# The first stage of a decoder step on one core: how the norm's weights arrive, which queue carries the small transfers, and where two row blocks are turned

## The chip, the core and the metric

The kernel runs on one core of a Trainium2 chip. The metric is the device time of one execution in microseconds (us). TensorE, VectorE, ScalarE and POOL (GpSimd) compute; SyncE, ScalarE and POOL issue DMA transfers, each on a queue of its own.

## The reference

One inference step of a hybrid decoder with 1024 prompt rows and 8 sampled sequences of 4 new rows, 1056 rows of width 1024 together. Only the beginning matters here:

```python
def rmsnorm(x, g):
    xf = x.astype(F32)
    y = xf * lax.rsqrt(jnp.mean(xf * xf, -1, keepdims=True) + EPS)
    return (y * g.astype(F32)).astype(x.dtype)
...
def mixer_inputs(x, g, w_in):
    B, T = x.shape[:2]
    proj = rmsnorm(x, g) @ w_in
...
def layer_tail(x, mix, w_out, g_mlp, w_up, w_down, g_ple, w_ple, w_ple_gate, p):
    x = x + mix @ w_out
```

The normed rows go through one projection, whose columns feed an attention group and a convolution group; behind them come output projection, MLP, an embedding term and a last norm. The raw `x` is needed again for the first residual.

## The kernel before

All is float32; a product is made of three matmuls of fp32r parts (high times high, high times low, low times high), so each operand is split into a high part (`..hi`, ScalarE) and a low part (`..lo`, VectorE here).

The first stage, function `front`, is one program per engine, in an order written out by hand; the engines meet at semaphores. The 1056 rows are nine blocks `x_rows0` to `x_rows8` (the last with 32 rows). For each block r: ScalarE squares and sums (`square`, L576) and takes the root (`root`, L581); VectorE makes the inverse and scales with the norm's weights `g_rows`, 128 partitions x 1024, into `xn` (`scale`, L1035, buffers of two); TensorE turns it in eight 128x128 transposes into the banks `ps_a` and `ps_b` (`side("xn..")`, L810); ScalarE copies the high part `Ahi` (`high`, L587) and VectorE subtracts the low part `Alo` (`low`, L1043), after which a bank is free.

`g_rows` is made on the chip: one row of 4 KB, `g_row`, is loaded, TensorE multiplies it with a column of ones (L862), and ScalarE copies the two banks (L678).

The projection has 19 tiles of 128 columns (`TILES`). Tile t is: weights `win_raw` loaded by SyncE (L179, one buffer), high part (L187), low part (L1083), 24 x 3 matmuls of 352 columns (L791), and an epilogue on ScalarE (or VectorE, L1078, for the kind "a"). Tiles 0 and 1 are run by thirds j of the rows, so that they begin when the first three blocks are turned; tiles 2 to 18 run whole. Into tiles 1 to 16 other turns are slotted, by the table `IN_TILE`: a `side` after the sixth, 13th and 20th group of matmuls.

The raw rows are also turned and sent to DRAM (`x_spill`) for the residual: eight transposes, two ScalarE copies and two DMA issues for each block (`keep_x`, L603 and L611). Blocks 6, 7, 8, 2, 3, 4, 5 use `ps_a` and `ps_b` within tiles 0 to 4 (`X_KEPT_ORDER`, `IN_TILE`). Blocks 0 and 1 are turned at the very start into banks that the projection needs only later (`first_rows`, L841); ScalarE copies them around the high part of tile 1's weights.

Fifteen small transfers (constants, page table, state rows, one pair of weights; the first is `g_row`) are issued by ScalarE before anything else (L557 to L569). TensorE turns the constants (L871 to L873) after the blocks 0 to 2, when nine of them have landed (`loaded`). VectorE, once it has `u`, works through 124 convolution taps between its other duties; POOL has its own taps for the sampled rows.

## Time and profile before

| | |
|---|---|
| median of 3 runs | 1925.12 us (1924.26 to 1925.91) |
| the profiled execution | 1924.49 us, span 1922.7 us |
| TensorE busy | 1845.2 us, 96% of the span |
| VectorE, ScalarE, POOL busy | 914.4, 664.1, 590.8 us |
| DMA | 163.67 MB, mean 85 GB/s |
| granted TensorE clock, mean | 0.985 of full |

The span runs from the first to the last instruction of the profiled execution. In rows of the profile a start is given in us from the beginning of the span, then a duration; rows of several instructions (x4) give the time that they cover. Names are those of the code without buffer numbers; L1035 is a line of the kernel. PEld is TensorE's weight load.

### The profile page before, as it was taken

What the parts mean: (1) busy time and instruction counts of PE and PEld (TensorE: products, weight loads), DVE (VectorE), ACT (ScalarE), POOL (GpSimd) and SP (SyncE); (2) the same over time, 40 slices, a digit from 0 to 9 for tenths busy, and PEclk for the clock granted to TensorE, in tenths of its full rate; (3) what the DMA queues carried; (4) which work ended last, traced back from release to release, by engine and by line L of the source; (5) the groups of instructions that cost most, each with busy time, mean ns of one, the idle gap of its engine ahead of it and who ended that gap; (6) DMA issues with size and microseconds to landing.
All of it is one profiled execution on the core that took longest, in us unless ns stands there. A gap on an engine that the chain in (4) does not pass through costs nothing.

```text
span 1922.7 us, 35068 instructions
## 1 busy us (share of the span) xinstructions
PE 1845.2 (96%) x13394; PEld 1724.5 (90%) x13394; DVE 914.4 (48%) x1622; ACT 664.1 (35%) x1249; POOL 590.8 (31%) x582
## 2 busy tenths in 40 slices
PE   7999998999988999999999999999999999999998
PEld 6999988999975767667999999999999999999898
DVE  5699965675538677766423221222221212124425
ACT  4312332345335666667222211121212121214335
POOL 0002962233214443434343222222222212125531
PEclk8999998999999999999999999999999999999999
DMA  5322455536322544441432111111111111112114
GB/s 159 91 62 59 108 173 139 137 105 160 97 90 62 146 128 122 122 133 56 135 109 76 34 44 44 45 44 55 34 55 39 50 40 50 39 45 94 50 39 135
DMA packets 195069, 163.67 MB, mean 85 GB/s; under 512 B 23157, under 2 KB 177474, under 8 KB 194384
## 3 DMA queue, kind: packets, MB, share of 16 engines
q1 hardware_dynamic: 176493, 139.11, 24.5%
q0 software_dynamic: 5568, 15.21, 3.1%
q10 hardware_dynamic: 12842, 7.09, 1.3%
q8 instruction: 111, 1.82, 0.4%
q14 instruction: 55, 0.44, 0.1%
HBM read 147.70 MB, written 18.25 MB: 86 GB/s over the span
## 4 chain that ended last, share of the span: by engine, by line
PE 30%; issue 25%; POOL 9%; DVE 4%; ACT 2%; POOLq 0%; DVEq 0%; ACTq 0%
PE ps L206 10%; POOL wm_lo L192 6%; PE ps L2219 5%; PE ps L2591 4%; PE ps L1663 2%; PE ps L1675 2%; PE ps L1652 2%; POOL S L1619 2%; DVE S L1919 1%; PE ps L1702 1%; PE ps L2608 1%; PE ps L1710 1%; ACT S L1802 1%; PE ps L1738 1%; DVE y_lo L2084 0%
## 5 line engine op out<-in xcount | busy, mean ns | idle before, releaser
L192 POOL TENSOR_TENSOR wm_lo<-wm_raw,wm_hi 128x512 fp32r<-128x512 f32 (+1 forms) x96 | 169.0, 1760 | 557.3 <-ACT wm_hi L187 557.3
L2408 DVE TENSOR_TENSOR xT<-ps,xT 128x1056 f32<-128x1056 f32 x64 | 80.5, 1258 | 260.1 <-PE ps L206 260.1
L1619 POOL TENSOR_SCALAR S<-S,inv,gate_p 128x64 f32<-128x64 f32 (+6 forms) x192 | 122.8, 657 | 195.7 <-DVE inv L1929 195.7
L187 ACT ACTIVATE wm_hi<-wm_raw 128x512 fp32r<-128x512 f32 (+1 forms) x96 | 73.9, 769 | 286.6 <-PE ps L206 286.6
L206 PE MATMUL ps<-Ahi,wm_hi 128*128 128x352 f32 x768 | 167.5, 326 | 4.5 <-POOL wm_lo L192 2.5
L206 PE MATMUL ps<-Hhi,wm_hi 128*128 128x352 f32 x768 | 167.3, 326 | 1.3 <-POOL wm_lo L192 1.3
L206 PE MATMUL ps<-Ahi,wm_lo 128*128 128x352 f32 x768 | 166.2, 324 | 0.0
L206 PE MATMUL ps<-Alo,wm_hi 128*128 128x352 f32 x768 | 165.8, 324 | 0.0
L206 PE MATMUL ps<-Hhi,wm_lo 128*128 128x352 f32 x768 | 165.6, 323 | 0.0
L206 PE MATMUL ps<-Hlo,wm_hi 128*128 128x352 f32 x768 | 165.3, 323 | 0.0
L936 PE MATMUL ps_p<-Xhi,w1hi 128*128 128x256 f32 x544 | 159.1, 293 | 1.5 <-ACT Xhi L665 1.5
L1066 DVE SCALAR_TENSOR_TENSOR y<-u,conv_w,y 128x1024 f32<-128x1024 f32 x120 | 156.5, 1350 | 1.2
L936 PE MATMUL ps_p<-Xhi,w1lo 128*128 128x256 f32 x544 | 153.2, 282 | 0.0
L936 PE MATMUL ps_p<-Xlo,w1hi 128*128 128x256 f32 x544 | 152.8, 283 | 0.0
L2389 DVE SCALAR_TENSOR_TENSOR sq<-ps,rstd 128x1056 f32<-128x1056 f32 x32 | 40.2, 1258 | 233.6 <-PE ps L206 233.6
L206 PEld LDWEIGHTS ps<-Ahi,wm_hi 128*128 128x128 f32 x768 | 131.4, 190 | 5.8 <-POOL wm_lo L192 2.7
L2318 ACT ACTIVATE sq<-sq 128x1056 f32<-128x1056 f32 x32 | 34.8, 1087 | 294.5 <-DVE sq L2389 294.5
L206 PEld LDWEIGHTS ps<-Hhi,wm_hi 128*128 128x128 f32 x768 | 130.3, 189 | 3.4 <-POOL wm_lo L192 3.4
L206 PEld LDWEIGHTS ps<-Ahi,wm_lo 128*128 128x128 f32 x768 | 132.4, 188 | 0.0
L206 PEld LDWEIGHTS ps<-Hhi,wm_lo 128*128 128x128 f32 x768 | 131.9, 188 | 0.0
L206 PEld LDWEIGHTS ps<-Alo,wm_hi 128*128 128x128 f32 x768 | 130.8, 188 | 0.0
L206 PEld LDWEIGHTS ps<-Hlo,wm_hi 128*128 128x128 f32 x768 | 130.4, 188 | 0.0
(383 smaller groups left out, 3908.5 us busy)
## 6 DMA issues: line engine op xcount, KB each, us to landing
s_raw<-in_cache_slc_kv_dram SPq DMA_DIRECT2D x256, 128.0 KB, 2.1
raw<-in_cache_cmp_kv_dram SPq DMA_DIRECT2D x140, 128.0 KB, 4.3
wm_raw<-in_w_up_dram SPq DMA_DIRECT2D x32, 512.0 KB, 4.0
wm_raw<-in_w_down_dram SPq DMA_DIRECT2D x64, 256.0 KB, 2.6
raw<-in_cache_cmp_kv_dram POOLq DMA_DIRECT2D x116, 128.0 KB, 4.5
win_raw<-in_w_in_dram SPq DMA_DIRECT2D x38, 256.0 KB, 3.4
wg_raw<-in_w_ple_gate_dram SPq DMA_DIRECT2D x14, 512.0 KB, 3.8
xT<-x_spill SPq DMA_DIRECT2D x2, 2112.0 KB, 11.0
```

Of the source, the lines that this page charges most:

```text
L187: self.c.nc.scalar.activation(self.hi[s][:, 0:nk, :], self.raw[rs][:, 0:nk, :], ACT.Copy).then_inc(self.hi_ready, 1)
L192: self.c.nc.gpsimd.tensor_tensor(self.lo[s][:, 0:nk, :], self.raw[s % self.raw_slots][:, 0:nk, :], self.hi[s][:, 0:nk, :].bitcast(F32), AL ...
L206: mm = nc.tensor.matmul(ps[:, j, 0:CH], w[s][:, k, :], x(k)[:, CH * j:CH * j + CH], start=(k == 0 and n == 0), stop=(k == nk - 1 and n == 2))
L936: mm = nc.tensor.matmul(ps_h[n % 2][:, 0:w], ws[cc][:, j, :], x[n % 2][:, j % 8, slice(j // 8, j // 8 + w)], start=(j == 0 and m == 0), st ...
L1066: i = V_.scalar_tensor_tensor(out=y, in0=x, scalar=w, in1=y, op0=ALU.mult, op1=ALU.add)
L1619: nc.gpsimd.tensor_scalar(x, x, inv[:, n % 3, 3 * e + br:3 * e + br + 1], c.gate_p[:, i, H * br + h:H * br + h + 1], ALU.mult, ALU.mult).t ...
L1652: mm = nc.tensor.matmul(ps_S[:, s + e, off:off + w], c.q[rows, g, P * i:P * i + P], keys, start=True, stop=True)
L1663: mm = nc.tensor.transpose(ps[:, P * (2 * j + e):P * (2 * j + e) + P], S[UNITS[n][1]][:, e, col:col + P], c.ident[:])
L2219: mm = nc.tensor.matmul(banks[t % 2][:, j, 0:CH], w[t % 2][:, k, :], x(k)[:, CH * j:CH * j + CH], start=(n == 0 and m == 0), stop=(n == KT ...
L2389: nc.vector.scalar_tensor_tensor(out=three(sq[s][:]), in0=banks[s][:, :, 0:CH], scalar=0.0, in1=three(c.rstd[:]), op0=ALU.max, op1=ALU.mul ...
L2408: nc.vector.tensor_tensor(three(x), banks[s][:, :, 0:CH], three(x), ALU.add).then_inc(W.free, 1)
L2591: mm = nc.tensor.matmul(ps[:, bank, 0:a1 - a0], w[t % 2][:, k, :], x[:, k, a0:a1], start=(k == 0 and m == 0), stop=(k == KT - 1 and m == 2))
```

## The change

The row of weights is no longer spread by TensorE: one DMA, issued by ScalarE as its only transfer in front, reads `g_attn` 128 times and writes all of `g_rows` (512 KB). The other fourteen transfers of ScalarE's list (into `t_rows`, `t_conv`, `pe_rows`, `pages`, `state_rows` and `w2`) are issued by POOL, after its memsets. `first_rows` is gone; blocks 0 and 1 are turned like the others, last in the order, block 0 in tile 4 and block 1 in tile 5.

```diff
--- before.py
+++ after.py
@@ -230,9 +230,9 @@
 NT = len(TILES)
 NR = QB + 1
 X_BATCHES = ((0, 1, 2), (3, 4, 5), (6, 7, 8))
-X_KEPT_ORDER = (0, 1, 6, 7, 8, 2, 3, 4, 5)
-AUX = ([f"xn{r}" for r in range(NR)] + [f"xT{r}" for r in X_KEPT_ORDER[2:]] + ["state", "conv"] + [f"rows{r}" for r in range(NR)] + ["gate"])
-IN_TILE = {1: ("xT6", "xT7"), 2: ("xT8", "xT2"), 3: ("xT3", "xT4"), 4: ("xT5",), 6: ("state",), 12: ("conv",),
+X_KEPT_ORDER = (6, 7, 8, 2, 3, 4, 5, 0, 1)
+AUX = ([f"xn{r}" for r in range(NR)] + [f"xT{r}" for r in X_KEPT_ORDER] + ["state", "conv"] + [f"rows{r}" for r in range(NR)] + ["gate"])
+IN_TILE = {1: ("xT6", "xT7"), 2: ("xT8", "xT2"), 3: ("xT3", "xT4"), 4: ("xT5", "xT0"), 5: ("xT1",), 6: ("state",), 12: ("conv",),
...
@@ -315,7 +315,6 @@
     ss = c.at("x_sums", [P, NR], F32, REST_OFF + 1152)
     x_rstd = c.at("x_rstd", [P, NR], F32, REST_OFF + 1216)
     warm = c.at("warm", [P, 1], F32, REST_OFF + 1280)
-    g_row = c.at("g_row", [1, D], F32, W1_OFF + 7296 + 4096)
...
     loaded, made, masked, const_turned = c.sem("small_loaded"), c.sem("const_made"), c.sem("const_masked"), c.sem("const_turned")
     pages_loaded, state_loaded = c.sem("pages_loaded"), c.sem("state_loaded")
-    g_loaded, g_spread, g_kept, x_loaded = c.sem("g_loaded"), c.sem("g_spread"), c.sem("g_rows_kept"), [c.sem(f"x_rows_loaded{r}") for r in range(NR)]
+    g_loaded, x_loaded = c.sem("g_loaded"), [c.sem(f"x_rows_loaded{r}") for r in range(NR)]
     squared, x_var, x_root, x_inv, scaled = c.sem("x_squared"), c.sem("x_var"), c.sem("x_root"), c.sem("x_inverse"), c.sem("x_scaled")
-    x0_turned, x0_kept = c.sem("x_first_turned"), c.sem("x_first_kept")
...
@@ -515,6 +513,18 @@
             pool.wait_ge(made, 9)
             nc.gpsimd.memset(u[:, :, 0:HIST], 0.0).then_inc(u_zero, 1)
             nc.gpsimd.memset(c.QB[:], 0.0).then_inc(zeroed, 1)
+            for n, name in enumerate(("g_attn", "g_mlp", "g_ple")):
+                pool.dma_start(t_rows[n * KT:(n + 1) * KT, :], a[name].rearrange("o (k p) -> (o k) p", p=P)).then_inc(loaded, 16)
+            pool.dma_start(t_rows[3 * KT:4 * KT, :], a["g_final"].rearrange("(k p) -> k p", p=P)).then_inc(loaded, 16)
+            for n, name in enumerate(("conv_b", "ln_conv_g", "ln_conv_b")):
+                pool.dma_start(t_rows[32 + n * CT:32 + (n + 1) * CT, :], a[name].rearrange("o (k p) -> (o k) p", p=P)).then_inc(loaded, 16)
+            pool.dma_start(t_conv[:, :], a["conv_w"].rearrange("o w f -> (o w) f")).then_inc(loaded, 16)
+            pool.dma_start(pe_rows[:, :], a["pe_cmp"].rearrange("o c (j e) d -> (o c j) (e d)", e=2)).then_inc(loaded, 16)
+            pool.dma_start(c.pages[0:1, :], a["page_table"].rearrange("(o b) n -> o (b n)", o=1)).then_inc(pages_loaded, 16)
+            for s in range(2):
+                pool.dma_start(st_rows[s][0:4 * HIST, :], a["state_conv"][0, 4 * s:4 * s + 4].rearrange("b t f -> (b t) f")).then_inc(state_loaded, 16)
+            for cc in range(2):
+                pool.dma_start(w2[:, cc, :], a["w_cmp2"][0, cc]).then_inc(w2_loaded, 16)
             pool.wait_ge(scaled, NR)
             nc.gpsimd.memset(c.Vn[:], 0.0).then_inc(zeroed, 1)
             nc.gpsimd.memset(c.VcP[:], 0.0).then_inc(zeroed, 1)
@@ -554,19 +564,7 @@
 
         @block.scalar
         def _(act):
-            act.dma_start(g_row[:], a["g_attn"]).then_inc(g_loaded, 16)
-            for n, name in enumerate(("g_attn", "g_mlp", "g_ple")):
-                act.dma_start(t_rows[n * KT:(n + 1) * KT, :], a[name].rearrange("o (k p) -> (o k) p", p=P)).then_inc(loaded, 16)
...
-                act.dma_start(w2[:, cc, :], a["w_cmp2"][0, cc]).then_inc(w2_loaded, 16)
+            act.dma_start(g_rows[:], a["g_attn"].to_broadcast([P, D])).then_inc(g_loaded, 16)
 
             def square(r):
                 n = n_rows(r)
@@ -591,21 +589,12 @@
 
                 n, m = n_rows(r), X_KEPT_ORDER.index(r)
                 for half in range(2):
-                    if m < 2:
-                        act.wait_ge(x0_turned, 2 * m + half + 1)
-                        src = (ps0[:, 1, :], ps0[:, 2, :], ps1[:, 0, :], ps1[:, 1, :])[2 * m + half]
-                    else:
-                        act.wait_ge(turned[half], aux(f"xT{r}") + 1)
-                        src = small[half]
+                    act.wait_ge(turned[half], aux(f"xT{r}") + 1)
                     slot = 2 * (m % 2) + half
                     if m >= 2:
                         act.wait_ge(x_sent[slot], 16 * (m // 2))
-                    i = nc.scalar.activation(x_out[slot][:, :, 0:n], src[:, 0:4 * n].rearrange("p (k n) -> p k n", n=n), ACT.Copy)
-                    i.then_inc(x0_kept if m < 2 else read[half], 1)
-                if m < 2:
-                    act.wait_ge(x0_kept, 2 * m + 2)
-                else:
-                    both_read(act, f"xT{r}")
+                    nc.scalar.activation(x_out[slot][:, :, 0:n], small[half][:, 0:4 * n].rearrange("p (k n) -> p k n", n=n), ACT.Copy).then_inc(read[half], 1)
+                both_read(act, f"xT{r}")
                 for half in range(2):
                     slot = 2 * (m % 2) + half
                     act.dma_start(x_spill[:, 4 * half:4 * half + 4, P * r:P * r + n], x_out[slot][:, :, 0:n]).then_inc(x_sent[slot], 16)
@@ -673,9 +662,6 @@
 
             act.wait_ge(made, 5)
             nc.scalar.activation(warm[:], c.eps[:], ACT.Sqrt)
-            act.wait_ge(g_spread, 2)
-            for half in range(2):
-                nc.scalar.activation(g_rows[:, 512 * half:512 * half + 512], small[half][:], ACT.Copy).then_inc(g_kept, 1)
             for batch in X_BATCHES:
                 square(batch[0])
                 root(batch[0])
@@ -687,9 +673,7 @@
                     if r == 0:
                         W.split_hi(act, 0, 0, 2)
                     elif r == 2:
-                        keep_x(0)
                         W.split_hi(act, 1, 1, 2)
-                        keep_x(1)
             keep_x(6)
             epilogue(0)
             W.split_hi(act, 2, 0, 2)
@@ -833,14 +817,6 @@
                             mm = nc.tensor.transpose(small[half][0:n, P * m:P * m + P], c.proj[:, t, P * r:P * r + n], c.ident[:])
                         mm.then_inc(turned[half], 1)
 
-            def first_rows(r):
-                pe.wait_ge(x_loaded[r], 16)
-                for half in range(2):
-                    bank = (ps0[:, 1, :], ps0[:, 2, :], ps1[:, 0, :], ps1[:, 1, :])[2 * r + half]
-                    for k in range(4):
-                        mm = nc.tensor.transpose(bank[:, P * k:P * k + P], x_rows[r][:, P * (4 * half + k):P * (4 * half + k) + P], c.ident[:])
-                    mm.then_inc(x0_turned, 1)
-
...
@@ -857,13 +833,7 @@
                     mm.then_inc(pages_turned, 1)
 
             pe.wait_ge(made, 5)
-            pe.wait_ge(g_loaded, 16)
-            for half in range(2):
-                nc.tensor.matmul(small[half][:], c.ones[0:1, :], g_row[:, 512 * half:512 * half + 512], start=True, stop=True).then_inc(g_spread, 1)
-            first_rows(0)
-            pe.wait_ge(g_kept, 2)
             side("xn0")
-            first_rows(1)
             side("xn1")
             side("xn2")
             pe.wait_ge(loaded, 9 * 16)
@@ -880,8 +850,6 @@
                 for t in range(2):
                     if j == 0:
                         pe.wait_ge(W.lo_ready, t + 1)
-                        if t:
-                            pe.wait_ge(x0_kept, 4)
                     for m in range(NG):
                         mm = group(t, m, (j,))
                         if j == NCH - 1 and m == NG - 1:
@@ -1031,7 +999,7 @@
                 if r >= 2:
                     dve.wait_ge(turned[1], aux(f"xn{r - 2}") + 1)
                 if r == 0:
-                    dve.wait_ge(g_kept, 2)
+                    dve.wait_ge(g_loaded, 16)
                 V_.scalar_tensor_tensor(out=xn[r % 2][0:n, :], in0=x_rows[r][0:n, :], scalar=x_rstd[0:n, r:r + 1], in1=g_rows[0:n, :],
                                         op0=ALU.mult, op1=ALU.mult).then_inc(scaled, 1)
 
```

The front of TensorE's list before, up to the constants; `ps_a` and `ps_b` are the two banks, `ps_p` the projection's, `x_rows_86` and `_87` blocks 0 and 1, `xn_78` and `_79` the two buffers of scaled rows:

```order
L862 MATMUL ps_a<-g_row,ones 128x512
L862 MATMUL ps_b<-g_row,ones 128x512
L841 MATMUL ps_p<-ident,x_rows_86 128x128 x8
L810 MATMUL ps_a<-ident,xn_78 128x128 x4
L810 MATMUL ps_b<-ident,xn_78 128x128 x4
L841 MATMUL ps_p<-ident,x_rows_87 128x128 x8
L810 MATMUL ps_a<-ident,xn_79 128x128 x4
L810 MATMUL ps_b<-ident,xn_79 128x128 x4
L810 MATMUL ps_a<-ident,xn_78 128x128 x4
L810 MATMUL ps_b<-ident,xn_78 128x128 x4
```

The same place after the change:

```order
L794 MATMUL ps_a<-ident,xn_78 128x128 x4
L794 MATMUL ps_b<-ident,xn_78 128x128 x4
L794 MATMUL ps_a<-ident,xn_79 128x128 x4
L794 MATMUL ps_b<-ident,xn_79 128x128 x4
L794 MATMUL ps_a<-ident,xn_78 128x128 x4
L794 MATMUL ps_b<-ident,xn_78 128x128 x4
L841 MATMUL ps_p<-ident,t_conv 128x31 x4
```

The two matmuls that spread the weights and both groups of eight raw transposes are gone; three scaled blocks in a row are left.

The front of ScalarE's list before, from the end of its transfers to the first high part (`w_77` is `w2`):

```order
L567 DMA state_rows_106<-in_state_conv_dram 120x512
L569 DMA w_77<-in_w_cmp_dram 128x64 x2
L675 ACT_TABLE_LOAD
L675 ACTIVATE warm<-eps 128x1
L678 ACTIVATE g_rows<-ps_a 128x512
L678 ACTIVATE g_rows<-ps_b 128x512
L576 ACTIVATE x_squares,x_sums<-x_rows_86 128x1024
L581 ACTIVATE x_rstd<-x_rstd 128x1
L576 ACTIVATE x_squares,x_sums<-x_rows_87 128x1024
L581 ACTIVATE x_rstd<-x_rstd 128x1
L587 ACTIVATE Ahi<-ps_a 128x4x128
```

And after (`win_hi_139` is the high part of tile 0's weights):

```order
L567 DMA g_rows<-in_g_attn_dram 128x1024
L664 ACT_TABLE_LOAD
L664 ACTIVATE warm<-eps 128x1
L574 ACTIVATE x_squares,x_sums<-x_rows_86 128x1024
L579 ACTIVATE x_rstd<-x_rstd 128x1
L574 ACTIVATE x_squares,x_sums<-x_rows_87 128x1024
L579 ACTIVATE x_rstd<-x_rstd 128x1
L585 ACTIVATE Ahi<-ps_a 128x4x128
L585 ACTIVATE Ahi<-ps_b 128x4x128
L187 ACTIVATE win_hi_139<-win_raw_138 128x1024
L574 ACTIVATE x_squares,x_sums<-x_rows_88 128x1024
```

In front of the table load one transfer stands instead of fifteen, and between the table load and the first square the copies into `g_rows` are gone.

ScalarE's list before in the tiles 4 and 5, between the epilogue of tile 3 (`u`, L641) and that of tile 5 (`proj`, L643); `x_out` are the copies of turned raw rows, whose transposes stand at the same places of TensorE's list:

```order
L641 ACTIVATE u<-ps_p 128x1056
L187 ACTIVATE win_hi_141<-win_raw_139 128x1024
L603 ACTIVATE x_out_107<-ps_a 128x512
L603 ACTIVATE x_out_108<-ps_b 128x512
L611 DMA x_spill<-x_out_107 128x4x128
L611 DMA x_spill<-x_out_108 128x4x128
L187 ACTIVATE win_hi_140<-win_raw_139 128x1024
L643 ACTIVATE proj<-ps_p 128x1056
```

After, from the `win_hi` behind the epilogue of tile 3 on:

```order
L187 ACTIVATE win_hi_140<-win_raw_138 128x1024
L596 ACTIVATE x_out_107<-ps_a 128x512
L596 ACTIVATE x_out_108<-ps_b 128x512
L600 DMA x_spill<-x_out_107 128x4x128
L600 DMA x_spill<-x_out_108 128x4x128
L596 ACTIVATE x_out_109<-ps_a 128x512
L596 ACTIVATE x_out_110<-ps_b 128x512
L600 DMA x_spill<-x_out_109 128x4x128
L600 DMA x_spill<-x_out_110 128x4x128
L187 ACTIVATE win_hi_139<-win_raw_138 128x1024
L596 ACTIVATE x_out_107<-ps_a 128x512
L596 ACTIVATE x_out_108<-ps_b 128x512
```

Behind the copies of block 5 those of block 0 are new, in tile 4; those of block 1 follow behind the `win_hi` of the next tile, in tile 5. Each stands for eight more transposes on TensorE in that tile.

## Rows read from the trace of the kernel before

**Rows 1.** Busy us (x instructions) of each engine by stretch, then TensorE's alone.

```profile
core 0: us, PE busy (x) PEld busy (x) DVE busy (x) ACT busy (x) POOL busy (x), PEclk, DMA share, GB/s
...
80.00:260.00 180.00, 180.00 (x1147) 179.47 (x1146) 171.72 (x134) 44.76 (x77) 78.64 (x63) 1.00 0.31 86
260.00:300.00 40.00, 28.22 (x192) 27.51 (x191) 17.76 (x34) 10.96 (x23) 15.32 (x23) 0.87 0.67 185
...
20.00:24.00 4.00, 3.45 (x16) 0.50 0.92 320
```

**Rows 2.** Timeline of ScalarE, front: start us, us, instruction, [idle before <-releaser].

```profile
6.13 0.92 ACTq L569 DMA_DIRECT2D w<-in_w_cmp_dram  x2
7.08 1.28 ACT L675 ACT_TABLE_LOAD   x1 [7.08 <-issue]
...
9.44 1.06 ACT L576 ACTIVATE x_squares<-x_rows 128x1024 f32<-128x1024 f32 x1
...
15.15 1.05 ACT L187 ACTIVATE win_hi<-win_raw 128x1024 fp32r<-128x1024 f32 x1
...
24.60 1.06 ACT L187 ACTIVATE win_hi<-win_raw 128x1024 fp32r<-128x1024 f32 x1 [1.04 <-issue]
```

**Rows 3.** Timeline of VectorE, front: the scaling of row blocks 0 and 3.

```profile
11.24 1.28 DVE L1035 SCALAR_TENSOR_TENSOR xn<-x_rows,x_rstd,g_rows 128x1024 f32<-128x1024 f32 x1
...
29.50 1.29 DVE L1035 SCALAR_TENSOR_TENSOR xn<-x_rows,x_rstd,g_rows 128x1024 f32<-128x1024 f32 x1
```

**Rows 4.** Timeline of TensorE, front.

```profile
20.02 1.08 PE L810 MATMUL ps_a<-ident,xn 128*128 128x128 f32 x4 [2.83 <-DVE Alo L1043]
...
21.89 0.63 PE L871 MATMUL ps_p<-ident,t_conv 31*128 31x31 f32 x4
...
23.41 0.63 PE L791 MATMUL ps_p<-Ahi,win_hi 128*128 128x352 f32 x1 [0.53 <-issue]
...
31.24 0.60 PE L810 MATMUL ps_a<-ident,xn 128*128 128x128 f32 x4
...
36.69 1.09 PE L810 MATMUL ps_a<-ident,xn 128*128 128x128 f32 x4 [2.17 <-DVE Alo L1043]
```

**Rows 5.** SyncE's issues, then DMA landings by window 0:1, 2.3:2.8, 2.8:3.4 (last number).

```profile
2.37 1.07 SPq L179 DMA_DIRECT2D win_raw<-in_w_in_dram  x2
...
x_rows<-in_x_prompt_dram SPq DMA_DIRECT2D x1, 512.0 KB, 3.7
...
win_raw<-in_w_in_dram SPq DMA_DIRECT2D x1, 256.0 KB, 6.3
...
win_raw<-in_w_in_dram SPq DMA_DIRECT2D x1, 256.0 KB, 10.8
```

**Rows 6.** DMA packets, MB, share of 16 engines, windows 2:4, 4:6, 8:10.

```profile
q1 hardware_dynamic: 146, 0.56, 90.7%
...
DMA packets 240, 0.74 MB, mean 372 GB/s; under 512 B 40, under 2 KB 61, under 8 KB 240
...
q1 hardware_dynamic: 284, 0.37, 69.1%
q10 hardware_dynamic: 129, 0.22, 42.4%
```

**Rows 7.** Timeline of ScalarE, first instructions after tiles 2, 3, 4 and 5.

```profile
79.15 1.05 ACT L643 ACTIVATE proj<-ps_p 128x1056 f32<-128x1056 f32 x1 [4.68 <-PE ps_p L791]
...
92.48 1.05 ACT L641 ACTIVATE u<-ps_p 128x1056 f32<-128x1056 f32 x1 [4.66 <-PE ps_p L791]
...
105.03 1.07 ACT L187 ACTIVATE win_hi<-win_raw 128x1024 fp32r<-128x1024 f32 x1 [8.10 <-PE ps_p L791]
116.62 1.05 ACT L643 ACTIVATE proj<-ps_p 128x1056 f32<-128x1056 f32 x1 [10.53 <-PE ps_p L791]
```

**Rows 8.** Timeline of POOL; last, its DMA issues on the page (us to landing).

```profile
1.55 0.28 POOL L507 TENSOR_SCALAR_AFFINE_SELECT ident<-ident 128x128 f32<-128x128 f32 x1 [0.24 <-POOL x_sums L505]
...
2.60 0.31 POOL L517 MEMSET QB<- 128x256 f32 x1
...
297.33 2.27 POOL L411 DMA_DIRECT2D raw<-in_cache_cmp_kv_dram  x4 [7.03 <-issue]
...
327.66 3.38 POOL L411 DMA_DIRECT2D raw<-in_cache_cmp_kv_dram  x2 [24.11 <-DVE relaid L1133]
...
raw<-in_cache_cmp_kv_dram POOLq DMA_DIRECT2D x116, 128.0 KB, 4.5
```

More of the change, by code:

```diff
@@ L556, in _ @@
         def _(act):
-            act.dma_start(g_row[:], a["g_attn"]).then_inc(g_loaded, 16)
-            for n, name in enumerate(("g_attn", "g_mlp", "g_ple")):
-                act.dma_start(t_rows[n * KT:(n + 1) * KT, :], a[name].rearrange("o (k p) -> (o k) p", p=P)).then_inc(loaded, 16)
-            act.dma_start(t_rows[3 * KT:4 * KT, :], a["g_final"].rearrange("(k p) -> k p", p=P)).then_inc(loaded, 16)
-            for n, name in enumerate(("conv_b", "ln_conv_g", "ln_conv_b")):
-                act.dma_start(t_rows[32 + n * CT:32 + (n + 1) * CT, :], a[name].rearrange("o (k p) -> (o k) p", p=P)).then_inc(loaded, 16)
-            act.dma_start(t_conv[:, :], a["conv_w"].rearrange("o w f -> (o w) f")).then_inc(loaded, 16)
-            act.dma_start(pe_rows[:, :], a["pe_cmp"].rearrange("o c (j e) d -> (o c j) (e d)", e=2)).then_inc(loaded, 16)
-            act.dma_start(c.pages[0:1, :], a["page_table"].rearrange("(o b) n -> o (b n)", o=1)).then_inc(pages_loaded, 16)
-            for s in range(2):
-                act.dma_start(st_rows[s][0:4 * HIST, :], a["state_conv"][0, 4 * s:4 * s + 4].rearrange("b t f -> (b t) f")).then_inc(state_loaded, 16)
-            for cc in range(2):
-                act.dma_start(w2[:, cc, :], a["w_cmp2"][0, cc]).then_inc(w2_loaded, 16)
+            act.dma_start(g_rows[:], a["g_attn"].to_broadcast([P, D])).then_inc(g_loaded, 16)
             def square(r):
```

## The prediction

> **What bounds the kernel now.** The profiled execution took 1924.49 us, its span is 1922.7, so 1.8 us lie around the span; the median of the three runs shown, 1925.12, is 0.6 above the profiled one. I read first the busy time by stretch [rows 1]: TensorE is busy for all 180.00 us between 80 and 260, so in the projection from tile 3 on whatever lengthens TensorE's list lengthens the kernel. In 260 to 300 it is busy for 28.22 of 40 us; the waits there begin when the last projection tile ends, so they move with it and give nothing back. What is left to win is in front. There I read ScalarE's timeline [rows 2]: the queue of small transfers keeps ScalarE's sequencer until 7.05 (6.13 + 0.92), only then come the table load (7.08), the two copies of `g_rows` and the first square (9.44). From that square on the stage is one chain over three engines: xn0 on VectorE at 11.24 [rows 3], its transposes, `win_hi` at 15.15, the next square behind it, the transposes of xn2 at 20.02, and the first projection matmul at 23.41 [rows 2 to 4]. From the first square to the first projection matmul are 23.41 - 9.44 = 13.97 us.
>
> **The change, part by part.**
>
> *The weights of the norm.* ScalarE now issues one transfer in place of fifteen (the last pair took 0.92 / 2 = 0.46 each [rows 2]). Its table load then starts once POOL has made the identity, at 1.55 + 0.28 = 1.8 [rows 8], and with 1.28 us for it and 0.2 for the activation behind it ScalarE is free at 3.4. So the first square starts when x_rows0 has landed. Today that is 0.89 + 3.7 = 4.6 us [rows 5]. The new transfer is of 512 KB like x_rows0, issued at the same moment on the other queue. The transfers moved 0.74 MB between 4 and 6 us, 0.37 MB a us [rows 6]; another 0.52 MB at that rate is 1.4 us. I put the landing of both at 4.6 + 1.4 = 6.0. The square begins 9.44 - 6.0 = 3.4 us earlier, and xn0, which wants the weights 1.8 us behind the square (11.24 - 9.44), has them.
> The Trainium skill ("DMA: Bandwidth & Descriptors", "Issuing engines are not separate DMA queues") says that transfers run on the same 16 DMA engines and interleave whoever issued them. The rows agree: in 8 to 10 us the two queues took 69.1% and 42.4%, together the whole [rows 6]. Were they separate, x_rows0 would land at 4.6 still and the gain be 4.8; by the rule it is 3.4.
> Bounds: 4.8 from above (x_rows0 alone ahead). From below: the price of 128 reads of one 4 KB row is in no row. The slowest landing of the front stretch is that of the second half of `win_raw`, 10.8 us after issue [rows 5]; with that, the weights land at 0.9 + 10.8 = 11.7, xn0 begins 0.5 later than today and the gain is -0.5. I stay with 3.4, as the same size, the same 4 KB pieces and the same 128 partitions make x_rows0 the nearest row.
> x_rows1 comes 1.4 behind at 7.4, and the second square wants it at 6.0 + 1.5 = 7.5: no wait.
>
> *Does the rest of the chain follow?* It wants the first projection weights. `win_hi` starts at 15.15 today without waiting; 3.4 earlier is 11.7. The halves of `win_raw` were issued at 2.37 and about 2.9 and landed 6.3 and 10.8 us later, at 8.7 and 13.7 [rows 5]. Equal halves of one queue five us apart: something in the other queue held back a few of the DMA engines. That other queue carried the small transfers of ScalarE. They now go out from POOL: the first after its memset at 2.60 + 0.31 = 2.9 [rows 8], each taking 2.27 / 4 = 0.57 us or more to issue, so `t_conv`, the eighth, leaves at 6.9 at the earliest and the two state transfers, the largest, from 8.6. Then the second half follows the first by the 0.7 us that 0.26 MB take: 8.7 + 1.4 + 0.7 = 10.8, before 11.7. No wait taken. If instead it keeps its lag, it lands at 13.7 + 1.4 = 15.1 and the whole 3.4 is gone.
> [...]
>
> *TensorE's head.* The two matmuls that spread the weights and the 16 first transposes go. The chain didn't wait for them: the transposes of xn2 (20.02) waited for VectorE, the matmul at 23.41 too [rows 4]. Worth 0. They kept TensorE from idling, so the transposes of xn1 may come at the lower level, 1.09 instead of 0.60 us for four [rows 4]; xn1 has over 1 us to spare, since ScalarE takes it only after the square of row 2. xn2's are at 1.08 already, with a granted clock of 0.50 in 20 to 24 [rows 1]: nothing to lose.
>
> *ScalarE's copies of rows 0 and 1.* In front of `win_hi` of tile 1 (24.60, with 1.04 us of issue before it [rows 2]) stood one pair of copies and its two issues, and behind it another. Without them `win_hi` and the square of row 3 come some 2 and 4 us earlier relative to the first matmul. It buys nothing: xn3 was scaled at 29.50 + 1.29 = 30.8, and TensorE reached its transposes by its own list at 31.24 without a wait [rows 3, 4]. The idle time behind (xn5's transposes at 36.69, 2.17 us of waiting) hangs on ScalarE's copies of those xn3 transposes, and so on TensorE's place in its list. The next load, that of tile 1's weights, starts on the low part of tile 0, which also moves. Worth 0; if the stall at 36.69 shrank with it, up to 2.2 more.
>
> *Constants.* TensorE waits for nine of the moved transfers before the transposes at 21.89, then 18.5. Issued from 2.9, at 0.57 each, landed 4.5 later: 2.9 + 5.1 + 4.5 = 12.5. At the slowest pace of POOL's issues, 3.38 / 2 = 1.69: 22.6 [rows 8]. These transfers are smaller than the ones in both rows, so I take the fast end: hidden by 6 us. Behind the issues POOL only waits for all nine rows to be scaled, long after.
>
> *Rows 0 and 1 in tiles 4 and 5.* Two more groups of eight transposes inside stretches where TensorE never idles. ScalarE's epilogues give tile lengths [rows 7]: tile 3 with two groups 92.48 - 79.15 = 13.33, tile 5 with none 116.62 - 105.03 = 11.59, so 0.87 each: 1.7 us on the path. ScalarE's copies and issues (2 us each) lie beside it, as it is busy 44.76 of 180 [rows 1]. In the head the same transposes cost nothing.
>
> **Sum.** -3.4 + 1.7 = -1.7 us: 1924.49 - 1.7 = 1922.8 for the profiled execution, 1925.12 - 1.7 = **1923.4 us** for the median. I call within 0.2% (3.85 us) what a measurement of this kernel can't tell from no change; this is 0.09%.
>
> **The rivals.**
> - *The first weights of the projection keep their lag* (15.1): nothing gained, 1.7 paid, 1926.8. For it: 0.5 MB more traffic ahead of them, and all POOL issues fall before them too. Against: the lag has the look of a few DMA engines held up by the small transfers.
> - *Constants late from POOL.* At 22.6 the first projection matmul is 1.5 later (23.41 - 21.89), at 24.1: 0.7 lost plus 1.7, 1927.5. It begins to cost once they land after 18.5, and turns the kernel slower than before after 20.2.
> - *The broadcast is slow, and the kernel slower.* If reads of one HBM row are served one by one: the first queue's 146 packets took 90.7% of 16 engines for 2 us, 0.2 us each [rows 6]; 128 in a row are 25 us, the weights land at about 27, xn0 waits 16 us more than today: 1924.5 + 16 + 1.7, near 1943. It is slower than before once the weights land after 11.24 - 1.7 = 9.5, and measurably once they land after 13.4. Nothing in the trace reads one row twice at once, so neither for nor against; the 16 DMA engines were near full on distinct rows.
> - *More is won.* x_rows0 at 4.6 and the stall at 36.69 gone: 4.8 + 2.2 - 1.7 = 5.3 less, 1919.8. Against: TensorE reached xn3's place without a wait.
>
> **How the numbers follow.** Forecast (a gain of 0 to 3.1 in net) 0.60; late projection weights 0.17; late constants 0.08; slow broadcast 0.07, of which 0.05 measurable; more won 0.08, of which 0.05 measurable. Range: 1925.12 - 3.1 = 1922.0, with 1 us for the spread of the runs (1924.26 to 1925.91) 1921.0 below; above the two late cases, 1927.5. Faster by over 0.2% 0.05, within 0.89, slower 0.06.
>
> **What would show it.** First square at about 6.0, not 9.44; `win_hi` at about 11.7 without a DMA wait before it; no wait before the `t_conv` transposes; first projection matmul near 20.0; xn3's transposes near 27.8 and again no wait; tile 5 of 12.5 us instead of 11.59, tile 4 lengthened likewise; later stages the same, all 1.7 earlier. Wrong it would be by a DMA wait before xn0 or `win_hi`, by a stall of TensorE before the constants, or by the end not moving with tile 5.

## The result and the profile after

| | before | after |
|---|---|---|
| median | 1924.66 us (1920.30 to 1926.33, 8 runs) | 1931.61 us (1929.06 to 1933.14, 8 runs) |
| the profiled execution | 1924.49 us | 1932.27 us, span 1930.5 us |
| granted TensorE clock, mean | 0.985 | 0.983 |

The ratio is 1.0036 [1.0025, 1.0047]: 0.36% slower, 7 us, where 1.7 us less was forecast. The time lies above the range (1921.0 to 1927.5). The busy times hardly moved (TensorE 1845.9 us, VectorE 914.0, ScalarE 663.3), so what was added is mostly idle time.

The first square and the first projection matmul came as forecast. ScalarE's timeline after, which answers to [rows 2]:

```profile
1.34 1.28 ACT L664 ACT_TABLE_LOAD   x1 [1.34 <-PEq L2685]
...
6.14 1.06 ACT L574 ACTIVATE x_squares<-x_rows 128x1024 f32<-128x1024 f32 x1 [3.30 <-DMA x_rows<-in_x_prompt_dram]
...
11.84 1.05 ACT L187 ACTIVATE win_hi<-win_raw 128x1024 fp32r<-128x1024 f32 x1
```

The square waits for x_rows0 alone, and begins 3.30 us earlier; `win_hi` starts without a DMA wait. The halves of its raw weights landed 8.0 and 8.3 us after their issue, against 6.3 and 10.8 before, so the lag of the second half is gone. TensorE's timeline after, which answers to [rows 4]:

```profile
16.71 1.09 PE L794 MATMUL ps_a<-ident,xn 128*128 128x128 f32 x4 [2.81 <-DVE Alo L1011]
...
18.58 0.63 PE L841 MATMUL ps_p<-ident,t_conv 31*128 31x31 f32 x4
...
20.11 0.63 PE L775 MATMUL ps_p<-Ahi,win_hi 128*128 128x352 f32 x1 [0.53 <-issue]
...
28.35 0.60 PE L794 MATMUL ps_a<-ident,xn 128*128 128x128 f32 x4
```

No wait before the constants of POOL (`t_conv`), the first projection matmul at 20.11 instead of 23.41, xn3's transposes at 28.35 instead of 31.24. ScalarE's first instructions after tiles, which answer to [rows 7] (tile 3's epilogue began at 90.12):

```profile
103.51 1.07 ACT L187 ACTIVATE win_hi<-win_raw 128x1024 fp32r<-128x1024 f32 x1 [4.71 <-PE ps_p L775]
...
115.94 1.05 ACT L632 ACTIVATE proj<-ps_p 128x1056 f32<-128x1056 f32 x1 [8.04 <-PE ps_p L775]
```

Tile 4 took 103.51 - 90.12 = 13.39 us (12.55 before), tile 5 12.43 (11.59): 0.84 more each. So 0.68 us is won at the end of tile 5, and still at 277.07 (277.76 before). Then it turns over. The MLP, over 1000 us further on, is a loop (`eng.Fori`, three passes, L2242 after) in which TensorE jumps back twice. TensorE's timeline of before behind the two jumps:

```profile
1352.92 0.75 PE L206 MATMUL ps<-Ahi,wm_hi 128*128 128x352 f32 x3 [1.06 <-issue]
...
1541.54 0.75 PE L206 MATMUL ps<-Ahi,wm_hi 128*128 128x352 f32 x3 [0.98 <-issue]
```

and of after:

```profile
1353.47 0.75 PE L206 MATMUL ps<-Ahi,wm_hi 128*128 128x352 f32 x3 [0.72 <-issue]
1356.53 0.63 PE L206 MATMUL ps<-Alo,wm_hi 128*128 128x352 f32 x3 [2.31 <-issue]
1357.00 0.64 PE L206 MATMUL ps<-Ahi,wm_lo 128*128 128x352 f32 x3
...
1544.69 0.74 PE L206 MATMUL ps<-Ahi,wm_hi 128*128 128x352 f32 x3 [1.23 <-issue]
1547.47 1.04 PE L206 MATMUL ps<-Alo,wm_hi 128*128 128x352 f32 x3 [2.03 <-issue]
1548.31 1.08 PE L206 MATMUL ps<-Ahi,wm_lo 128*128 128x352 f32 x3
```

Before, each jump costs one wait of about 1 us "for issue", that is, for nothing which the profile shows. After, three matmuls run and a second wait of 2.31 and 2.03 us follows. Behind the second jump some 20 matmuls run at the lower of TensorE's two clock levels: three of them take 1.08 us instead of 0.65, until 1552.7.

Queue q8 carries TensorE's code. This is read from the traces: it is of the kind "instruction", and where TensorE never waits its packets come 20.3 us apart. What it moved in the whole execution, before and then after:

```profile
q8 instruction: 111, 1.82, 0.4%
```

```profile
q8 instruction: 113, 1.85, 0.4%
```

These are packets of 16 KB (1.82 MB / 111), and after the change there are two more of them, one for each jump. Their times in the trace show what the second wait is for. At a jump, in every kernel, one packet moves 2.6 to 3.2 us before TensorE starts the loop's first matmul (at 1350.8 after the change) and the next 3.1 to 4.2 us behind it (at 1353.9, done at 1355.2). Before the change nothing waits for the second packet. After it, the second wait ends at 1356.5, 1.3 us behind that packet's end; so it is in all ten second waits of this document (1.25 to 1.54 us).

The change has 10 instructions fewer in TensorE's list ahead of the loop: two fp32 matmuls, each of which the profile shows as two matmuls and two weight loads, and two waits. TensorE's time by windows, clock in the third column from the end, before and then after:

```profile
1530.00:1570.00 40.00, 39.02 (x242) 38.73 (x241) 7.75 (x7) 8.36 (x8) 8.65 (x5) 1.00 0.17 48
```

```profile
1530.00:1570.00 40.00, 36.74 (x211) 36.32 (x210) 6.29 (x5) 5.87 (x6) 8.56 (x4) 0.91 0.19 54
```

Lined up by ScalarE's instructions, after stands against before at -0.69 at 277, -0.19 at 301, -0.23 at 590, +1.26 at 609, +0.90 at 1352, +3.01 at 1366, +2.91 at 1541, +7.84 at 1555, and 7.8 at the end. The two jumps are 2.1 + 4.9 = 7.0 of the 8.5 us that were lost behind tile 5; 0.5 went between 277 and 301, and 1.5 between 590 and 609; 0.5 came back in small pieces.

### The profile page after: what moved, and what is told of

Read it like the earlier page. It is cut to its first block, busy times and chain, and to the rows that moved or that the text cites. A ratio compares the mean times of both kernels' runs of the same rounds, so it can differ in the third digit from the quotient of the medians.

```text
span 1930.5 us, 35058 instructions
## 1 busy us (share of the span) xinstructions
PE 1845.9 (96%) x13390; PEld 1726.8 (89%) x13390; DVE 914.0 (47%) x1622; ACT 663.3 (34%) x1247; POOL 597.8 (31%) x596
## 4 chain that ended last, share of the span: by engine, by line
PE 30%; issue 26%; POOL 9%; DVE 4%; ACT 2%; DMA 0%; POOLq 0%; SPq 0%; DVEq 0%; ACTq 0%
PE ps L206 10%; POOL wm_lo L192 6%; PE ps L2187 5%; PE ps L2559 3%; PE ps L1631 2%; PE ps L1643 2%; PE ps L1620 2%; POOL S L1587 2%; DVE S L1887 1%; PE ps L1670 1%; PE ps L2576 1%; PE ps L1678 1%; ACT S L1770 1%; PE ps L1706 1%; DVE y_lo L2052 0%
```

## The experiments

Medians of before: 1925.63 us in the first set of four (22 runs), 1924.78 in the second (34), 1924.89 in the third (28).
### First set: is it the place of the loop head?

**a_plus10**: the changed kernel, padded by the 10 instructions that it lost.

```diff
             pe.wait_ge(made, 5)
+            for _ in range(20):
+                pe.wait_ge(made, 5)
```

> The changed kernel with ten more instructions (waits that are already satisfied) ahead of TensorE's first transpose, where TensorE is idle until 9.37 us. Theory 1 (place in the code): the changed kernel has 10 fewer instructions in TensorE's list than before, and that puts the head of the MLP loop, to which TensorE jumps back twice, some 8 instructions ahead of a boundary at which the next 16 KB of code must be fetched. Ten more put the head back where it was. Expected: no second wait of about 2 us behind the loop's first matmuls, the two rounds 1.7 and 4.8 us shorter, 1931.6 - 6.5 = 1925.1 us; nearer 1923.5 if the 1 and 0.9 us lost at 296 and at 604 us come back as well. Theory 2 (timing or traffic: POOL's transfers, or the other times at which things happen): stays at 1931.6 with the waits of 2.3 and 2.0 us at the loop's head.

Measured: 1925.69 us (1923.70 to 1928.92, 11 runs), 1.0004 [0.9995, 1.0013]. Ten instructions that do nothing took 5.9 us away, by the medians of two sets. Its timeline behind the jumps:

```profile
1351.36 0.74 PE L206 MATMUL ps<-Ahi,wm_hi 128*128 128x352 f32 x3 [0.83 <-issue]
...
1539.62 0.75 PE L206 MATMUL ps<-Ahi,wm_hi 128*128 128x352 f32 x3 [0.72 <-issue]
```

The second waits are gone, three matmuls take 0.65 throughout, and q8 moves 111 packets, as before the change. It is 1.57 ahead of before at 1366 and 2.06 at 1902; then the last stage, at a granted clock of 0.78 from 1905 to 1925 against 0.98, gives the 2 us back.

**a_plus5**: the same with 10 waits, 5 instructions.

> The same with five more instructions instead of ten, as a control for the padding itself. Theory 1: the head then is some 3 instructions ahead of the boundary, the second wait comes earlier behind the jump and is as long, 1931.6 us (1930 to 1934). Theory 2, or an effect of waits in front as such: between the time of the changed kernel and that with ten, or no different from ten.

Measured: 1936.96 us (1933.69 to 1938.05, 5 runs), 1.0056 [1.0040, 1.0072]: slower than no padding.

```profile
1354.38 0.42 PE L206 MATMUL ps<-Ahi,wm_hi 128*128 128x352 f32 x1 [0.68 <-issue]
1357.57 0.95 PE L206 MATMUL ps<-Ahi,wm_hi 128*128 128x352 f32 x2 [2.77 <-issue]
...
1548.37 0.42 PE L206 MATMUL ps<-Ahi,wm_hi 128*128 128x352 f32 x1 [1.17 <-issue]
1551.60 0.95 PE L206 MATMUL ps<-Ahi,wm_hi 128*128 128x352 f32 x2 [2.80 <-issue]
```

One matmul runs before the second wait, not three: the boundary stood still and the head moved towards it. The waits are longer, as less work covers them, by 1.2 us together. The time is 5.4 us above what was expected, and beyond the range. In the trace the clock falls behind both jumps here (0.91 from 1345 to 1385, 1.00 in after), which costs 2.1 us more than in after, and again in the last stage, which costs 2.2.

**b_minus8**: the kernel before, with sixteen redundant waits (eight instructions) dropped from TensorE's list, and nothing else.

```diff
-                    pe.wait_ge(free[1], 7)
-                    pe.wait_ge(free[0], 7)
+                    if r not in (1, 2, 3, 4, 5, 6, 7, 8):
+                        pe.wait_ge(free[1], 7)
+                        pe.wait_ge(free[0], 7)
```

> The kernel before with eight instructions fewer in TensorE's list: of the two waits ahead of each block of output rows in the projection (free, 7, on both banks), which only the first can ever hold, those of blocks 1 to 8 are dropped. All work is the same. Theory 1: the loop's head comes to lie some 6 instructions ahead of the boundary, a second wait of over 2 us and a stretch at the lower clock follow each of the two jumps: about 6.5 us slower than before, 1931. Theory 2: no change, 1924.7 (within 1 us).

Measured: 1932.35 us (1928.31 to 1933.86, 8 runs), 1.0033 [1.0021, 1.0046]. None of the change's edits is in it, and the loss is that of the change: second waits of 2.66 and 2.42 us, each after two matmuls, and 113 packets of code:

```profile
1353.48 0.58 PE L206 MATMUL ps<-Ahi,wm_hi 128*128 128x352 f32 x2 [0.87 <-issue]
1356.72 0.45 PE L206 MATMUL ps<-Ahi,wm_hi 128*128 128x352 f32 x1 [2.66 <-issue]
...
1549.80 0.45 PE L206 MATMUL ps<-Ahi,wm_hi 128*128 128x352 f32 x1 [2.42 <-issue]
```

**front_turns**: broadcast and POOL's transfers of the change, but the raw rows 0 and 1 turned in front as before; padded to a_plus10's number of instructions.

> The change without its third part: blocks 0 and 1 are turned and copied in front as before, weights by one transfer and small transfers from POOL as in the changed kernel; TensorE's list padded by nine instructions, so that it has as many ahead of the loop as the kernel before. By the sum of the prediction the two groups of transposes in tiles 4 and 5 cost 1.7 us, and their absence in front brings nothing: expected 1.7 us less than the changed kernel with ten more instructions, about 1923.4, and 1.3 us less than before. Rival: the copies of blocks 0 and 1 and their issues on ScalarE (4 us) delay the weights of tile 1 and what follows, and cost in front what the tiles gain: same as with ten more instructions.

Measured: 1920.56 us (1916.11 to 1923.51, 9 runs), 0.9977 [0.9966, 0.9988]: faster than both kernels, and 2.8 us below what was expected. In the trace it is 2.79 ahead of before at 277 (274.97), where a_plus10 is level (277.76): the turns in tiles 4 and 5 give 1.7 of that. Another 3.0 us lie behind 1760, where the clock didn't fall. Windows of before, and then of front_turns:

```profile
1760.00:1790.00 30.00, 27.80 (x156) 26.80 (x155) 18.33 (x16) 14.81 (x13) 20.70 (x9) 0.94 0.18 54
1790.00:1820.00 30.00, 27.79 (x149) 27.25 (x149) 14.90 (x9) 9.14 (x11) 10.13 (x4) 0.94 0.18 53
```

```profile
1760.00:1790.00 30.00, 27.80 (x162) 26.59 (x161) 17.41 (x15) 15.03 (x13) 22.22 (x8) 1.00 0.22 66
1790.00:1820.00 30.00, 27.78 (x159) 27.46 (x158) 13.09 (x9) 8.62 (x10) 11.34 (x6) 1.00 0.13 39
```

Both have the same waits of 2.2 us there, for `wg_lo`. Each fall of the clock behind one costs 1.5 us.

### Second set: the parts of the front, and the place again

**pool_only**: the kernel before, with the fourteen small transfers behind `g_row` issued by POOL (the same lines, `act.dma_start` become `pool.dma_start`).

> The kernel before with one edit: the fourteen small transfers behind g_row are issued by POOL, as in the change; g_row stays one row of 4 KB that two matmuls spread, and the first raw rows are turned in front. TensorE's list has as many instructions as before, so the loop of the MLP lies where it lay. Theory (ScalarE's queue of issues was what held the first square): the table load starts at 1.3, the copies of g_rows wait for the two matmuls, of which the second ends at 6.15 in the kernel before, so the first square begins at about 6.8 in place of 9.44; behind the head all is some 2.2 earlier, near 1923.4 by the median of before (1925.6 in the last set). Rival (the broadcast is what brought front_turns its 5 us): within 1 us of before.

Measured: 1921.92 us (1918.73 to 1926.14, 12 runs), 0.9984 [0.9973, 0.9994].

```profile
6.28 0.60 ACT L678 ACTIVATE g_rows<-ps_a 128x512 f32<-128x512 f32 x1 [3.31 <-PE ps_b L862]
6.77 0.59 ACT L678 ACTIVATE g_rows<-ps_b 128x512 f32<-128x512 f32 x1
7.25 1.06 ACT L576 ACTIVATE x_squares<-x_rows 128x1024 f32<-128x1024 f32 x1
```

2.19 of the 3.30 us come from this move alone; the first square now stands behind two copies, not one as was expected (6.8). At 277 the kernel is 2.08 us ahead of before, as expected; the rival (no gain without the broadcast) falls.

**bcast**: the broadcast without the move; raw rows turned in front, padded like front_turns.

```diff
-            act.dma_start(g_row[:], a["g_attn"]).then_inc(g_loaded, 16)
+            act.dma_start(g_rows[:], a["g_attn"].to_broadcast([P, D])).then_inc(g_loaded, 16)
...
-            act.wait_ge(g_spread, 2)
-            for half in range(2):
-                nc.scalar.activation(g_rows[:, 512 * half:512 * half + 512], small[half][:], ACT.Copy).then_inc(g_kept, 1)
```

> The kernel before with the other half of the front's edit: g_rows comes by one transfer to 128 partitions, but the small transfers stay on ScalarE behind it; the first raw rows are turned in front; TensorE's list is padded with satisfied waits to the length of front_turns, so the loop head lies behind the block boundary. Theory (the queue of issues is what counts): ScalarE's sequencer is busy until about 7.0, the table load and the warm activation end at 8.5, the first square begins at 8.6, 0.8 earlier than before: 1924.8. Rival (the broadcast alone brings the gain of front_turns): 1920.6. If both were additive with the time of the last stages left to the clock, the spread around either is 2 us.

Measured: 1927.79 us (1922.44 to 1930.06, 12 runs), 1.0009 [0.9997, 1.0020]. The rival's 1920.6 is excluded; the theory's 1924.8 lies within the interval, though its mechanism was incomplete. The square began at 9.05 (8.6 expected), and then:

```profile
16.20 1.06 ACT L187 ACTIVATE win_hi<-win_raw 128x1024 fp32r<-128x1024 f32 x1 [1.42 <-DMA win_raw<-in_w_in_dram]
```

`win_hi` waits for its weights and begins 1.05 later than before, where front_turns, which differs in nothing but the queue of the small transfers, begins at 11.66 without a wait. That is the lag of [rows 5] again: the halves of `win_raw` landed 8.7 and 12.9 us after their issue here, 7.7 and 8.1 in front_turns. That the second is later than before (10.8) fits the 512 KB more ahead of it, but no run separates the two. At 277 the kernel is 2.2 us behind before.

**front_turns_raw**: front_turns without its padding.

> front_turns without its padding: nine instructions fewer in TensorE's list ahead of the loop of the MLP, nothing else. Theory (the head's place in the 16 KB block costs): a second wait for issue of 2 to 3 us behind each of the two jumps and some groups of matmuls at the lower clock behind them, 6 to 7 us more than front_turns, about 1927. Rival (after lost its time by another of its edits, the turns in tiles 4 and 5 or the copies with them): same as front_turns, 1920.6.

Measured: 1929.96 us (1923.83 to 1931.77, 11 runs), 1.0027 [1.0016, 1.0037]. Second waits of 1.95 and 2.28 us, and groups at 1.08 behind both; 9.4 above front_turns by the medians of two sets (6 to 7 were expected), 5.2 above before where front_turns is 5.1 below. The two jumps are 8.8 us of it. The turns in tiles 4 and 5 aren't in it, so they don't explain the loss of the change.

**a_plus40**: a_plus10's padding with 80 waits.

> The changed kernel with 80 satisfied waits in front of TensorE's list, which are 40 instructions: the loop head lies 30 instructions further on than in a_plus10. Theory (only a head shortly ahead of a block's end costs; any place from the block's begin on is as good): no second wait behind the jumps, 1925.7 as a_plus10. Rival (a_plus10 hit a lucky spot, or the first wait behind a jump grows with the distance into the block): between 1927 and 1932. If the waits themselves cost, the transposes of xn0 start after 9.37; up to 1 us of that would be seen at the end.

Measured: 1927.64 us (1925.35 to 1929.62, 12 runs), 1.0013 [1.0005, 1.0022]. No second wait (first ones of 0.67 and 0.96), as the theory said, and xn0's transposes wait for `xn` only (9.47), so the added waits are hidden. But it is 2 us above a_plus10. In the trace it loses 1.9 us to a_plus10 between 277 and 301, and 1.5 between 590 and 609. The windows of a_plus10 and then of after show the second place:

```profile
600.00:620.00 20.00, 17.60 (x187) 12.09 (x189) 17.20 (x58) 12.17 (x33) 9.33 (x13) 1.00 0.01 2
```

```profile
600.00:620.00 20.00, 17.60 (x145) 12.13 (x141) 15.60 (x53) 11.98 (x33) 9.34 (x13) 0.91 0.00 1
```

Near 604 TensorE runs eight transposes in 1.09 us in before and a_plus10, in 1.72 in after, 1.97 in a_plus40. Nothing waits longer there; the clock falls or doesn't.

### Third set: how far the bad places reach

**a_plus224**: the changed kernel with 448 waits, 200 in front and 248 where TensorE waits for `Xlo` at 286 to 295.

> The changed kernel with 448 satisfied waits, which are 224 instructions: 200 waits in front, the rest where TensorE waits 8.9 us for Xlo at 286 to 295. The loop head of the MLP then lies some 40 instructions ahead of the end of its 16 KB block (in the changed kernel some 8, in a_plus5 some 3, by the matmuls that run between the two waits). Theory (the second wait is the time to fetch the next block, less what the instructions up to the block's end take): packets of code come 20.3 us apart where TensorE never waits, 0.079 us for each of 256 instructions; 37 instructions more than in a_plus5, whose second waits were 2.77 and 2.80, cover 2.9 us, so no second wait: 1925.7 as a_plus10 plus whatever the added waits cost by 300 us. Rival (the second wait belongs to every head whose block ends within the loop's first matmuls, whatever the distance, or a_plus10 hit a lucky spot): a second wait of 2 us or more, 1931 to 1932.

Measured: 1929.19 us (1926.70 to 1930.93, 10 runs), 1.0022 [1.0013, 1.0031]. Behind the jumps one wait each (0.95 and 0.78), no second one: the theory holds. The time doesn't say so, because the padding isn't free: xn0's transposes start at 12.76 (issue), 3.4 late (so a wait takes some 0.05 us), and by 1366 the kernel is 4.8 behind a_plus10, of which 4.7 were lost by 301.

**a_plus240**: with 480 waits.

> The same with 480 waits, 240 instructions: the head some 24 instructions ahead of its block's end. Theory: 21 instructions more than in a_plus5 cover 21 x 0.079 = 1.7 of 2.8 us, so a second wait of about 1.1 us behind each jump, 24 instructions (about 8 to 10 matmuls) behind the first; 1.1 x 2 = 2.2 above a_plus224, and more only if TensorE's clock falls for it. Rival: as a_plus224, both with the same second wait.

Measured: 1930.94 us (1930.43 to 1933.42, 5 runs), 1.0034 [1.0022, 1.0047]. The second waits are back, behind eleven matmuls, and short:

```profile
1360.36 0.32 PE L206 MATMUL ps<-Ahi,wm_hi 128*128 128x352 f32 x1 [0.91 <-issue]
...
1550.16 0.32 PE L206 MATMUL ps<-Ahi,wm_hi 128*128 128x352 f32 x1 [1.46 <-issue]
```

1.1 was expected, 0.91 and 1.46 came (sum 2.4; the clock stays at 1.00). Eleven matmuls are 22 instructions of the 24. That 240 instructions more bring the second wait back, 16 further from the boundary than in after, is also what shows the blocks' length in instructions: 240 + 16 = 256.

All kernels in one table. The third column is the time lost around each jump, with ScalarE's instructions lined up against before at 1352 and 1366, and at 1541 and 1555:

| instructions from loop head to block end | second wait behind the two jumps | lost around them | q8 packets | kernel |
|---|---|---|---|---|
| 3 | 2.77, 2.80 | 4.9, 5.8 | 113 | a_plus5 |
| 6 | 2.66, 2.42 | 4.9, 3.7 | 113 | b_minus8 |
| 7 | 1.95, 2.28 | 3.9, 4.9 | 113 | front_turns_raw |
| 8 | 2.31, 2.03 | 2.1, 4.9 | 113 | after |
| 24 | 0.91, 1.46 | 0.8, 1.3 | 113 | a_plus240 |
| 40 | none | -0.2, -0.2 | 113 | a_plus224 |
| head behind the boundary | none | -0.4 to 0.1 | 111 | before, a_plus10, a_plus40, b_plus10, front_turns, bcast, late_bcast, pool_only |

The steps between kernels are exact, as they are counted in TensorE's lists; where the boundary lies is read from the matmuls that run ahead of the second wait, to within an instruction or so. a_plus224 has the two more packets and no second wait: a block more to fetch costs nothing where the rest of the first one covers it. What is lost beyond the waits is the lower clock behind them, 1.5 to 2.6 us where it falls. It falls behind seven of the eight waits of 1.95 us and more, and behind neither of a_plus240.

**b_plus10**: the kernel before with 20 waits in front.

> The kernel before with 20 satisfied waits (10 instructions) in front of TensorE's list: a control for what the padding itself does. Theory: the head lies 10 instructions further behind the block's begin, no second wait, same as before within 1 us (1925). Rival (front_turns gained by its padding, or the head of before still costs something where it lies): about 1920 to 1922.

Measured: 1925.91 us (1921.73 to 1927.91, 12 runs), 1.0002 [0.9994, 1.0011]. Padding as such gives and costs nothing beyond 1 us.

**late_bcast**: front_turns, with the broadcast issued behind the warm activation.

```diff
-            act.dma_start(g_rows[:], a["g_attn"].to_broadcast([P, D])).then_inc(g_loaded, 16)
...
             nc.scalar.activation(warm[:], c.eps[:], ACT.Sqrt)
+            act.dma_start(g_rows[:], a["g_attn"].to_broadcast([P, D])).then_inc(g_loaded, 16)
```

> front_turns with the one transfer of g_rows issued behind ScalarE's table load and warm activation, at about 2.8, in place of 0.88, so that x_rows0 has the DMA engines to itself. Theory (the two transfers shared the 16 DMA engines, which put x_rows0 at 6.1 to 6.3 instead of 4.6): the first square begins at 4.7 to 5.0; xn0 then waits for the weights, which land 4.5 to 5.4 behind their issue, at 7.3 to 8.2; xn0 at 7.3 to 8.2 against 7.9 to 8.0, so the end moves by -0.6 to +0.2: 1920.6 as front_turns. Rival (x_rows0 lands at 6 whatever else is under way): first square at 6.1 still.

Measured: 1922.67 us (1920.02 to 1925.53, 11 runs), 0.9991 [0.9983, 1.0000].

```profile
4.61 1.06 ACT L574 ACTIVATE x_squares<-x_rows 128x1024 f32<-128x1024 f32 x1 [2.23 <-DMA x_rows<-in_x_prompt_dram]
```

```profile
9.21 1.28 DVE L1029 SCALAR_TENSOR_TENSOR xn<-x_rows,x_rstd,g_rows 128x1024 f32<-128x1024 f32 x1 [2.83 <-DMA g_rows<-in_g_attn_dram]
```

ScalarE's sequencer issued it at 1.87, ahead of the activation's end. x_rows0 alone lands at 4.6, so it is the broadcast that holds it until 6.1 (the rival falls); but the broadcast now lands 7.2 us after its issue, later than the 4.5 to 5.4 that were expected, and xn0 starts 1.3 later than in after. The kernel is 2.1 us slower than the 1920.6 expected: by 277 it is 1.0 behind front_turns.

## Why the prediction was wrong

- **The weights of the norm, -3.4: right.** The square began at 6.14, where 6.0 was forecast. The table load before it began at 1.34, not at 1.8, which costs nothing. The two transfers share the DMA engines: 4.61 without the other (late_bcast), 6.02 to 6.31 with it, some 1.5 us, where 1.4 was worked out. The rows named for it, 69.1% and 42.4%, show this less well than the text has it: they add up to 111.5%, so packet times overlap in them. 128 reads of one row took no longer than x_rows0 (5.4 and 5.2 us to landing), so the slow broadcast falls (its price of 1924.5 + 16 + 1.7 is 1942, not 1943).
- **The rest of the chain follows: right.** `win_hi` at 11.84 (11.7) without a wait, and the reason given, the small transfers on ScalarE's queue, is borne out by bcast against front_turns. How they held back half of the weights isn't shown. The margin was thin: that half landed at about 11.4, where 10.8 was worked out.
- **Constants: right**, hidden: they wait for nothing at 18.58.
- **Turns in tiles 4 and 5, +1.7: right**, 0.84 each.
- **The head as a whole was 1.0 too large.** Of 3.30 at the square and the first matmul, 2.89 are left at xn3's transposes and 2.36 at tile 3. The forecast carried the 3.4 through unchanged; the trace shows that TensorE's clock took most of the difference. Behind the first projection matmul TensorE ran 12 matmuls at the lower level (0.50 us each) after, 9 before; up to tile 3 there were six more of them in all, some 0.8 us. In a_plus10 there were still more, 16 instead of 12 behind that matmul; its lead at 277 is 0.7 us smaller than that of after. Why the clock rose when it did no run settles. The forecast also says that the matmul at 23.41 waited for VectorE; its row says "issue", and the wait was 0.53 us in both kernels.
- **The step that failed: "later stages the same, all 1.7 earlier".** The gain in front of the later stages was small (0.68 at 277), and they weren't the same. Ten instructions fewer in TensorE's list put the head of the MLP's loop 8 instructions ahead of the end of a 16 KB block of code. Behind each of the two jumps TensorE runs the rest of that block and then waits for the next one: 2.31 and 2.03 us, and a slower clock behind the second, 7.0 us in all. The prediction had no term for the place of the code: it put everything behind the front at nothing. This is shown in both directions, by a_plus10 and b_minus8, as a function of the distance by the table, and by the packets of code, behind which every second wait ends. The Trainium skill ("Runtime: NRT & Kernel Launch", "Instruction fetch mechanics") has the parts of it: blocks of 16 KiB with 256 instructions, fetched in sequence, and a fetch when a taken branch leaves the window. The trace agrees on the 16 KB and on a wait behind each jump (about 1 us in before).
- **Also not the same: the clock.** In stretches where TensorE waits a microsecond or two, its granted clock falls in some executions and kernels and stays in others (0.91 against 1.00 at 600 to 620, 0.94 against 1.00 at 1760 to 1820, 0.78 against 0.98 in the last 20 us, and 0.66 in before and after against 1.00 in front_turns_raw at 920 to 930). Each costs 1.5 to 2.5 us. Why one kernel falls at 604 and another not isn't settled; nor is how much of front_turns' 5 us is due to it. The medians of many runs include it, and a difference of 2 us between two kernels is therefore not safely that of their edits.
- **Size of the edits themselves.** With the head behind the boundary the change is worth nothing (a_plus10, 1.0004), since what the front gives (1.68 us at tile 3 in this trace) is paid in tiles 4 and 5. Without the turns in the tiles it measured 0.23% faster (front_turns), of which 2.8 us of 1925, 0.15%, are there at 277 in its trace; the rest goes with the clock behind 1760.

None of the rivals had this in it: all of them, like the forecast, looked for the price of an edit where the edit is.

## What to carry to other kernels

An edit of a few instructions moves every later loop head within its block of code; if a kernel with a hardware loop changes by some microseconds and nothing near the edit explains it, look behind the jumps for a second wait "for issue", count the instructions removed ahead of the loop, and pad the list by as many before judging the edit. Moving small DMA issues off the engine that starts the first computation was worth more here (2.1 us at 277) than the clever load, which alone lost 2.2 there and takes bandwidth from what is waited for first. The turns of two blocks cost their full length, 0.84 us each, in tiles where TensorE never idles, and nothing that these runs show in front, where it does.

## What the runs showed of the hardware

- A jump back costs TensorE 0.6 to 1.2 us by itself, and up to 2.8 more where its target lies 3 instructions ahead of the end of a 16 KB block; at 24 instructions it is 0.9 to 1.5, at 40 nothing. 256 instructions of these matmuls take about 20 us (a packet each 20.3 us), so by estimate 2.8 us are some 35 instructions.
- At a jump two packets of code move 3.1 to 4.2 us apart, and a second wait ends 1.25 to 1.54 us behind the end of the second one, in ten of ten.
- A wait that is satisfied takes TensorE about 0.05 us, by estimate: 200 of them, from some 2 us on, held xn0's transposes until 12.76; 80 were hidden ahead of 9.47.
- One transfer that reads a 4 KB row 128 times (512 KB) landed 5.4 us after its issue, beside an equal one of distinct rows at 5.2.
- POOL issued small transfers at 0.52 us each, ScalarE at 0.29 to 0.37, each apart from its first (0.74 and 0.54). POOL's landed 4.7 to 5.7 us after issue, the two of state rows and those of `w2` 8.0 to 8.5.
